# Nine norms of a three-block network: the sum of squares on every partition, the power on 128x256, no spread and no copy

## What is computed

```python
def rms_norm(x, g):
    xf = x.astype(jnp.float32)
    y = xf * lax.rsqrt(jnp.mean(xf * xf, axis=-1, keepdims=True) + EPS)
    return (y * g.astype(jnp.float32)).astype(x.dtype)

def sqrelu_mlp(x, w_up, w_down):
    h = jax.nn.relu(x @ w_up)
    return (h * h) @ w_down

for i in range(DEPTH):                       # the norms of the first two layers
    h = rms_norm(x, g[0]);  h = mixer(h, ...)
    x = x + rms_norm(h, g[1])
    h = sqrelu_mlp(rms_norm(x, g[2]), w_mlp_up[i], w_mlp_down[i])
    x = x + rms_norm(h, g[3])
```

## Time and profile before

| | before |
|---|---|
| median of 3 runs | 969.54 us |
| the profiled execution | 972.56 us |
| its span, first to last instruction | 970.4 us |
| TensorE matmuls busy | 955.5 us, 98% |
| VectorE (DVE) busy | 642.3 us, 66% |
| ScalarE (ACT) busy | 536.0 us, 55% |
| GpSimd (POOL) busy | 103.9 us, 11% |
| granted TensorE clock, mean | 0.993 |

### The profile page before, as it was taken

How to read it: one execution, slowest core, us unless ns; L and a number is a source line. 1 busy time by engine, 2 the same in 40 slices (tenths; PEclk the granted TensorE clock), 3 DMA queues, 4 the chain that set the end, 5 groups by cost and what they waited for, 6 DMA issues and landing times.

```text
span 970.4 us, 20173 instructions
## 1 busy us (share of the span) xinstructions
PE 955.5 (98%) x8074; PEld 947.1 (98%) x8074; DVE 642.3 (66%) x878; ACT 536.0 (55%) x757; POOL 103.9 (11%) x96
## 2 busy tenths in 40 slices
PE   9999999999999999999999999999999999999997
PEld 9999999999999999999999999999999999999997
DVE  5667677665444887588664444884765679999642
ACT  6566657654444555556565444556454566666442
POOL 0121100000010000119100000024020210000001
PEclk9899999999999999999999999999999999999999
DMA  9533645565555455536555555544443545554521
GB/s 349 197 131 101 211 167 210 181 200 190 204 186 179 149 200 188 198 131 218 209 180 211 180 179 192 200 161 138 153 147 126 174 157 191 201 188 173 201 104 44
DMA packets 26420, 172.17 MB, mean 177 GB/s; under 512 B 3444, under 2 KB 4084, under 8 KB 6136
## 3 DMA queue, kind: packets, MB, share of 16 engines
q1 hardware_dynamic: 26072, 171.04, 50.4%
q10 hardware_dynamic: 288, 0.27, 0.1%
HBM read 170.24 MB, written 1.05 MB: 177 GB/s over the span
## 4 chain that ended last, share of the span: by engine, by line
PE 82%; DVE 3%; ACT 2%; issue 1%; POOL 1%; POOLq 0%; DVEq 0%; ACTq 0%
PE po L433 24%; PE po L434 24%; PE po L435 24%; DVE wL L1357 1%; PE third L433 1%; PE third L434 1%; PE third L435 1%; PE po L461 1%; PE po L462 1%; PE po L460 1%; ACT wH L873 1%; POOL rtok L1963 1%; PE pn L523 1%; PE pc L791 1%; PE pn L533 0%
## 5 line engine op out<-in xcount | busy, mean ns | idle before, releaser
L1357 DVE TENSOR_TENSOR wL<-raw,wH 128x1024 fp32r<-128x1024 f32 x316 | 385.9, 1243 | 160.6 <-ACT wH L873 160.3
L873 ACT ACTIVATE wH<-raw 128x1024 fp32r<-128x1024 f32 x316 | 332.0, 1058 | 252.6 <-PE po L435 228.5
L433 PE MATMUL po<-xnH,wH 128*128 128x256 f32 x1296 | 365.7, 282 | 4.5 <-DVE rq L1395 2.2
L434 PE MATMUL po<-xnL,wH 128*128 128x256 f32 x1296 | 361.4, 279 | 0.0
L435 PE MATMUL po<-xnH,wL 128*128 128x256 f32 x1296 | 361.2, 279 | 0.0
L433 PEld LDWEIGHTS po<-xnH,wH 128*128 128x128 f32 x1296 | 246.1, 190 | 5.8 <-DVE xnL L1364 2.8
L434 PEld LDWEIGHTS po<-xnL,wH 128*128 128x128 f32 x1296 | 244.3, 188 | 0.2
L435 PEld LDWEIGHTS po<-xnH,wL 128*128 128x128 f32 x1296 | 244.2, 188 | 0.0
L435 PE MATMUL po<-hH,wL 128*128 128x256 f32 x688 | 190.8, 277 | 0.0
L433 PE MATMUL po<-hH,wH 128*128 128x256 f32 x688 | 190.8, 277 | 0.0
L434 PE MATMUL po<-hL,wH 128*128 128x256 f32 x688 | 190.8, 277 | 0.0
(11 more groups left out here) (307 smaller groups left out, 1157.1 us busy)
## 6 DMA issues: line engine op xcount, KB each, us to landing
raw<-in_weights SPq DMA_DIRECT2D x157, 1024.0 KB, 4.8
raw<-in_weights SPq DMA_DIRECT2D x4, 256.0 KB, 5.3
raw<-in_weights SPq DMA_DIRECT2D x2, 512.0 KB, 7.1
mem<-in_memT SPq DMA_DIRECT2D x1, 1024.0 KB, 12.6
out<-y SPq DMA_DIRECT2D x4, 256.0 KB, 2.6
x<-in_xT SPq DMA_DIRECT2D x3, 256.0 KB, 5.1
decayt<-in_decay SPq DMA_DIRECT2D x1, 512.0 KB, 3.4
x<-in_xT ACTq DMA_DIRECT2D x1, 256.0 KB, 4.8
```

What stands on the lines that cost most here:

```text
L433: pe.matmul(psum[:, n, 0:T], wH[w][:, wc], aH[:, ac, :], start=start, stop=False)
L434: pe.matmul(psum[:, n, 0:T], wH[w][:, wc], aL[:, ac, :], start=False, stop=False)
L873: act.activation(wH[b % HL][:, hs], raw[b % RAW][:, hs], ACT.Copy).then_inc(s_hi, 1)
L1357: dve.tensor_tensor(wL[b % HL][:, hs], raw[b % RAW][:, hs], wH[b % HL][:, hs].bitcast(f32), ALU.subtract)\
```

## The change

Nine norms (2 to 8, 10 and 11, called wide) take another way to R. Norms 0, 1, 9 and 12 keep the old one, since others need their 128x2 factor or since it is the last.

- `norm_sums`: the 128x128 ones are the stationary operand and the squares move, 128 columns at a time. The sum then stands on all partitions, 128x256 in `pn[:, 128:384]`. The number of matmuls is the same.
- `mean_square`: DVE computes 128x256 and writes it to a new tile `Rw` in SBUF.
- `factor`: GpSimd raises 128x256 to -0.5, in place for a "post" norm and into `Rs` for a "pre" norm.
- `norm_spread` and `keep_R` return at once. `boundary` waits for the power and reads `Rw`.
- The unused tile `spare` goes, and the counts in the waits are redone (`powers`, `spreads`).

```diff
@@ norm_sums (TensorE)
-                    if NORMS[n - 1] in ("pre", "preV"):
+                    if wide(n - 1):
+                        pe.wait_ge(s_ms, n)
+                    elif NORMS[n - 1] in ("pre", "preV"):
                         pe.wait_ge(s_Rs, pre)
...
-                        mm = pe.matmul(pn[:, t:t + 1], chunk, ones[:, 0:1], start=k == 0, stop=k == len(squared) - 1)
+                        if wide(n):
+                            mm = pe.matmul(pn[:, P + t * P:P + (t + 1) * P], ones[:, :], chunk, start=k == 0, stop=k == len(squared) - 1)
+                        else:
+                            mm = pe.matmul(pn[:, t:t + 1], chunk, ones[:, 0:1], start=k == 0, stop=k == len(squared) - 1)
@@ norm_spread (TensorE)
+                if wide(n):
+                    return
...
-                pe.wait_ge(s_r, n + 1)
+                pe.wait_ge(s_r, powers(n + 1))
@@ keep_R (ScalarE)
-                act.wait_ge(s_R, n + 1)
+                if wide(n):
+                    return
+                act.wait_ge(s_R, spreads(n + 1))
@@ mean_square (VectorE)
                 dve.wait_ge(s_sum, n + 1)
+                if wide(n):
+                    dve.tensor_scalar(Rw, pn[:, 128:128 + T], 1.0 / D, EPS, ALU.mult, ALU.add).then_inc(s_ms, 1)
+                    return
@@ boundary (VectorE), and the same for lines 1580 and 1582
-                dve.wait_ge(s_R, n + 1)
+                dve.wait_ge(s_r, powers(n + 1))
...
-                    dve.tensor_tensor(ys, ys, over_pair(pn[:, 128:128 + T]), ALU.mult).then_inc(s_t, 1)
+                    dve.tensor_tensor(ys, ys, over_pair(Rw), ALU.mult).then_inc(s_t, 1)
@@ factor (GpSimd)
                 pool.wait_ge(s_ms, n + 1)
+                if wide(n):
+                    half = minus_half[:, 0:1].to_broadcast([P, T])
+                    if NORMS[n] == "post":
+                        pool.tensor_tensor(Rw, Rw, half, ALU.pow).then_inc(s_r, 1)
+                    else:
+                        pool.tensor_tensor(Rs[:, :], Rw, half, ALU.pow).then_inc(s_Rs, 1)
+                    return
```

More of the change, by code:

```diff
@@ L115, in build @@
         Rm = sb("Rm", [P, T], f32)
-        spare = sb("spare", [P, TT, P], f32)
+        Rw = sb("Rw", [P, T], f32)[:, :]
         scratch = place[0]
@@ L339, in squares_summed, with wide, powers, spreads @@
             return sum(k == "preV" for k in NORMS[:norm])
+        def wide(n):
+            return n in (2, 3, 4, 5, 6, 7, 8, 10, 11)
+        def powers(norm):
+            return sum(not (wide(m) and NORMS[m] in ("pre", "preV")) for m in range(norm))
+        def spreads(norm):
+            return sum(not wide(m) for m in range(norm))
         def group_done(p):
@@ L919, in keep_values @@
                 psum = group(name, i)
-                act.wait_ge(s_r, norm_done)
+                act.wait_ge(s_r, powers(norm_done))
                 for t in range(TT):
@@ L1578, in add @@
                     dve.tensor_tensor(xs, xs, ys, ALU.add).then_inc(s_xadd, 1)
-                link(dve.tensor_tensor(y[:, 0, :], y[:, 0, :], pn[:, 128:128 + T], ALU.mult))
+                link(dve.tensor_tensor(y[:, 0, :], y[:, 0, :], Rw, ALU.mult))
                 dve.tensor_tensor(x[:, 0, :], x[:, 0, :], y[:, 0, :], ALU.add).then_inc(s_xadd, 1)
-                dve.tensor_tensor(y[:, 1, :], y[:, 1, :], pn[:, 128:128 + T], ALU.mult).then_inc(s_t, 1)
+                dve.tensor_tensor(y[:, 1, :], y[:, 1, :], Rw, ALU.mult).then_inc(s_t, 1)
                 dve.wait_ge(s_t, 4 * post + 1)
@@ L1926, in _ @@
             dve.tensor_scalar(ms[:, :], third[:, :, 0], 1.0 / D, EPS, ALU.mult, ALU.add).then_inc(s_ms, 1)
-            dve.wait_ge(s_R, 13)
+            dve.wait_ge(s_R, spreads(13))
             for p in range(3):
```

## The result

| | before | after |
|---|---|---|
| time, us, median (lowest to highest) | 970.34 (967.44 to 972.35) | 1329.66 (1327.35 to 1337.34) |
| ratio, 95% interval | | 1.3789 (1.3721 to 1.3857) |
| span of the profiled execution, us | 970.4 | 1325.3 |
| mean granted clock of TensorE | 0.993 | 0.859 |

Each median is of four executions, the three of the first table and one more for the kernel before. Forecast were 1347 us (own range 1300 to 1400); the time is 17 us under it.

The account below looks back on a forecast made before the run. TensorE's queue was taken to bound the kernel (98% of the span); nine long powers make it wait 363 us, plus 14 of clock: +377 on 972.56 gives 1349.6, less 3.0 for the median, 1347 us; own range 1300 to 1400, 8 in 10 1030 to 1430.

Parts of the forecast that it names:

- The power's length: GpSimd's power on 256 columns at each wide norm: 0.70 + 254 x 0.162 = 41.8 us; forecast's chance 0.70.
- The bounds of 1.1 and 65 us: GpSimd's power: 1.1 us if columns stream like an addition, 65 at 0.255 a column.
- the rival of overlapping columns: GpSimd's power partly pipelined on long rows, 4 to 30 us; 1055 us in all at 10; chance 0.14.
- Who waits: TensorE waits some 36 to 41 us nine times for `relu`, `cx`, `xq`, `apad` and `xnL`.
- The port: Shared SBUF port: a long GpSimd power holds it throughout, so VectorE's splits stand still until the power ends.
- The lower end of its range: 1300 us: no clock cost and port not held up, less 14 and about 30.
- the sign for this: In the changed profile: powers of 42 us with undisturbed splits would show that the port isn't held.
- The clock: TensorE restarts at granted clock 0.50 behind each of nine waits, 1.5 us lost each: 14 us.
- Spreads, sums, mean square: TensorE and VectorE at the norms: spreads take off 6.0 us, sums add 0.8, mean square goes from 0.16 to 0.38.
- the rival with 964.3 us: Power streams and reads inputs in gaps; gain is 6.0 us of spreads and waits less 0.8; chance 0.10.
- the one with 970: Power streams like an addition, 1.1 us, but holds the port: +0.7 us, 970; chance 0.06.
- the sum on the profiled execution: Whole kernel: 363 us of waits and 14 of clock, +377 on 972.56, gives 1349.6 us.

Follow-up runs that it names:

- the row of widths: No network: GpSimd powers of 128x2 to 128x256 with nothing beside them; a straight line, 0.160 us a column, 41.23 us for 256.
- the repeated test: Changed kernel with 162 to 179 idle matmuls in each of the nine waits, ending 0.4 us before the wait does: 1323.94 us, ratio 1.3689.
- the shift of three: Kernel before with three idle matmuls of 128 columns on TensorE behind the second slab of norm 11: 964.89 us, ratio 0.9980.
- shifted by 128 columns: Kernel before with one idle matmul of 128 columns on TensorE behind the second slab of norm 11: 966.30 us, ratio 0.9977.
- 64 columns: Kernel before with one idle matmul of 64 columns on TensorE behind the second slab of norm 11: 967.62 us, ratio 0.9992.

## Why the prediction was right, step by step

- **The power's length**: right, and it decided all. 41.8 us forecast from two small powers, 0.162 a column; 41.2 alone, 0.160 a column, 42.04 in the network. The bounds of 1.1 and 65 us and the rival of overlapping columns fell with the row of widths.
- **Who waits**: right. Nine waits, for `relu` (two), `cx`, `xq`, `apad`, `xnL` and, three times, behind the fillers, the longest of each kind 36.7 to 40.7 us.
- **The port**: wrong. The step "VectorE's other two half splits, held up, take 2.3 us", and 1.15 where one was left, was in all nine norms: 3 x 2.3 + 6 x 1.15 = 13.8 us too much. I had read the exclusion from an addition and powers of two columns, and carried it to a power that runs for 42 us. The first two show who comes in first; neither is long enough to show how long a power keeps VectorE out. It is 0.4 us (3.90 against 3.49 us for three splits, 1.64 against 1.22 for one). The prediction had a row that speaks against a power that blocks, norm 3's splits of 1.16 us each beside a power of 1.61, and used it for a rival only. The lower end of its range took off about 30 us for a port that isn't held; in its own sum the step is worth 13.8. The prediction named the sign for this, powers of 42 us with undisturbed splits, and it came.
- **The clock**: right in kind, perhaps a little high: 14 us forecast, 10 to 12 estimated from the repeated test.
- **Spreads, sums, mean square**: right that they decide nothing beside the power. The chain of waits, the view of the earlier trace rows, has 1.35 us for twelve sums (1.3 forecast) and 0.46 for four (0.44 forecast); the mean square takes 0.42 (0.38 forecast). The 6 us that the spreads took off would not have been a gain: without the power the rest measures 0.3 to 1.0% slower, so the rival with 964.3 us would have missed too, and the one with 970 is nearer.
- **The rest of the miss**: the sum on the profiled execution was 1349.6, that of the changed kernel took 1327.35. Of the 22.3 us, 13.8 are the port; 5.8 are the last stretch, 173.6 us against 179.4; about 3 stood in the part ahead of norm 2, which no edit touches, where norm 2's power starts at 120.6 instead of 123.6. That part was the granted clock, which fell to 0.50 between 24 and 32 us in the profile before and not in the profile after, first before, then after:

```profile
26.00:28.00 2.00, 2.00 (x10) 2.00 (x11) 0.37 (x1) 0.00 (x0) 0.00 (x0) 0.50 0.91 369
```

```profile
26.00:28.00 2.00, 2.00 (x20) 2.00 (x19) 0.69 (x2) 0.92 (x3) 0.00 (x0) 1.00 0.95 377
```

  The three make 22.6. The last two could not be forecast from one profile.

## What to carry to other kernels

Price an operation on a wide tile from two widths of the same operation, never from a sibling: on GpSimd a product of 128x256 costs 0.6 us and a power 41. Do such a function while the tile is narrow (here on 128x2) and spread the result; the spread costs TensorE 0.4 to 0.7 us, the wide function costs 40. And where two engines exclude each other, ask for how long: a short instruction shows that they do, only a long one shows until when.

## What the runs showed of the hardware

- **Two distances between matmuls at one clock.** With TensorE's queue full and the granted clock at 1.00, matmuls of 128x256 follow at 0.113 us in some stretches and 0.118 in others, 4% apart, and keep it over 150 us and more. Ten microseconds of the last stretch, unchanged and with the shift of three (count of matmuls behind PE's busy time):

```profile
850.00:860.00 10.00, 10.00 (x87) 10.00 (x87) 9.25 (x16) 6.14 (x9) 0.00 (x0) 1.00 0.61 210
```

```profile
850.00:860.00 10.00, 10.00 (x91) 10.00 (x89) 9.68 (x16) 6.65 (x9) 0.00 (x0) 1.00 0.55 184
```

  (A window also counts the matmuls that overlap its ends.) It changes where norms or attention break into the row. Two profiles of the kernel before have every stretch behind norm 2 alike, to 0.1 us, but the spans of its other executions fall into two groups 6 to 7 us apart at the same granted clock (957.9 to 958.9 and 965.0 to 965.1 us at 0.998), so it is most likely no fixed trait of the program. It is worth 6 us in the last stretch, about half of the scatter of this kernel's times (958 to 970 us of span in 25 executions), and a change should be judged by stretches at equal distance. What sets it stayed open.
- **The granted clock ahead of norm 2 is another part of the scatter.** In five profiles the code up to there is the same: the stretch from norm 1's power to norm 2's takes 98.9, 97.3, 95.8, 98.9 and 95.8 us, with a mean clock from 24 to 40 us of 0.79, 0.89, 1.00, 0.79 and 1.00 (the kernel before twice, then shifted by 128 columns, 64 columns and three times 128). It falls there in some executions although TensorE is busy all through.
- **GpSimd can be shut out for long.** An instruction on 16 columns took 8.26 us beside a dense row of VectorE's subtractions; with nothing beside it a like one took 0.26. It is one instance; the powers of two columns in the kernel before, which came just as a row of three splits began, took 1.61 us.
